# Moving two weight roundings and a bank copy ahead of the last hidden high part at every second turn of the weights

## The reference

```
def swiglu(h, wg, wu, wd):
    return (jax.nn.silu(h @ wg) * (h @ wu)) @ wd

h = rmsnorm(x, p['norm_ffn_pre'][l]) * (1 + sc_f) + sh_f
f = swiglu(h, p['w_ffn_gate'][l], p['w_ffn_up'][l], p['w_ffn_down'][l])
```

## Time and profile before

| | |
|---|---|
| median of 3 runs | 3141.03 us (3135.26 to 3142.76) |
| the profiled execution's own time | 3142.86 us |
| its span, first to last instruction | 3141.1 us |
| TensorE busy | 2906.9 us, 93% of the span |
| VectorE / ScalarE / GpSimd busy | 1744.2 / 1084.2 / 1271.5 us |
| seven-product units, layer 0 | 1214.9 to about 1650 us |
| seven-product units, layer 1 | 2389.0 to about 2825 us |

### The profile page before, as it was taken

One profiled execution on the slowest core, in us unless ns is written; L12 is line 12 of the kernel. 1 busy time (PEld: TensorE's weight loads), 2 busy tenths in 40 slices (PEclk: granted clock), 3 DMA queues, 4 the chain that ended last, 5 costly groups with the idle time before them and its releaser, 6 DMA issues. The chain is left out here.

```text
span 3141.1 us, 60389 instructions
## 1 busy us (share of the span) xinstructions
PE 2906.9 (93%) x24873; PEld 2617.4 (83%) x24873; DVE 1744.2 (56%) x3025; ACT 1084.2 (35%) x2178; POOL 1271.5 (40%) x899
## 2 busy tenths in 40 slices
PE   6999899899899898999999998898888999999997
PEld 4888576566566898999999997888888999999996
DVE  4331245465556477666654237787477666664234
ACT  5411136421112454333331015575464333331012
POOL 2411157633333453444443114586553444443112
PEclk8999989888889999999999999999999999999998
DMA  9455300255554332233237322311332223247322
GB/s 313 165 201 181 103 22 1 91 178 180 182 182 162 96 99 70 98 111 106 90 131 259 130 85 83 87 29 30 90 107 70 93 102 111 85 140 249 140 79 79
DMA packets 241597, 377.89 MB, mean 120 GB/s; under 512 B 15530, under 2 KB 156203, under 8 KB 241060
## 3 DMA queue, kind: packets, MB, share of 16 engines
q1 hardware_dynamic: 200092, 253.95, 24.5%
q0 software_dynamic: 20992, 75.51, 7.2%
q10 hardware_dynamic: 20240, 44.57, 3.9%
HBM read 298.71 MB, written 73.28 MB: 118 GB/s over the span
## 5 line engine op out<-in xcount | busy, mean ns | idle before, releaser
L791 PE MATMUL ps<-HS,w_split 128*128 128x272 f32 x1920 | 269.6, 290 | 12.4 <-ACT sg L1048 10.0
L807 PE MATMUL ps<-HS,w_ring 128*128 128x272 f32 x1920 | 274.7, 290 | 0.0
L791 PEld LDWEIGHTS ps<-HS,w_split 128*128 128x128 f32 x1920 | 250.6, 188 | 17.5 <-ACT sg L1048 14.6
L807 PEld LDWEIGHTS ps<-HS,w_ring 128*128 128x128 f32 x1920 | 255.5, 190 | 0.0
L2312 PEld LDWEIGHTS ps<-HS_in,w_split 128*128 128x128 f32 x1728 | 222.5, 191 | 27.7 <-issue 16.4
L2312 PE MATMUL ps<-HS_in,w_split 128*128 128x272 f32 x1728 | 233.4, 294 | 9.2 <-DVE HS_in L2531 9.1
L1786 DVE TENSOR_TENSOR Y<-Y,ps 128x272 f32<-128x272 f32 x256 | 112.1, 438 | 224.7 <-PE ps L807 224.7
L1384 POOL TENSOR_TENSOR w_split<-w_raw,w_split 128x512 fp32r<-128x512 f32 x120 | 170.0, 1430 | 120.9 <-ACT w_split L1040 120.9
L762 PE MATMUL ps<-HS,w_ring 128*128 128x272 f32 x1344 | 186.4, 301 | 26.5 <-PEq L156 12.1
L762 PEld LDWEIGHTS ps<-HS,w_ring 128*128 128x128 f32 x1344 | 182.1, 200 | 28.7 <-issue 13.6
L1384 POOL TENSOR_TENSOR w_ring<-w_raw,w_ring 128x512 fp32r<-128x512 f32 x40 | 61.9, 1547 | 282.6 <-ACT w_ring L1040 282.6
(11 more groups left out here) (496 smaller groups left out, 6702.0 us busy)
## 6 DMA issues: line engine op xcount, KB each, us to landing
hid_spill<-hid SPq DMA_DIRECT2D x40, 1088.0 KB, 7.4
w_mod_half<-w_mod_in SPq DMA_DIRECT2D x40, 1024.0 KB
HS<-hid_spill ACTq DMA_DIRECT2D x32, 1088.0 KB, 11.4
w_raw<-w_ffn_gate_in SPq DMA_DIRECT2D x44, 512.0 KB
w_raw<-w_ffn_up_in SPq DMA_DIRECT2D x44, 512.0 KB, 6.0
w_raw<-w_ffn_down_in SPq DMA_DIRECT2D x44, 512.0 KB
x_part<-x_spill SPq DMA_DIRECT2D x54, 272.0 KB, 3.0
x_spill<-Y SPq DMA_DIRECT2D x12, 1088.0 KB, 5.5
```

What stands on the lines that cost most here:

```text
L791: ins = pe.matmul(psum(U.banks(u)[b]), part_slot(j, a)[:, k, :], token_part(n, j, e)[:, k, :], start=(j < 3 and k == 0 and i == 0), stop=( ...
L807: ins = pe.matmul(down_bank(n), slots[DOWN_SLOT[t]][:, a, d * P:(d + 1) * P], hid_cols(k, t, q)[:, e, :], start=(t == lo and j == 0), stop ...
```

## The change

At the turns from an up unit to a gate unit (nine in a layer, after units 3, 7, ... 35; the set `EARLY_COPY` holds the gate unit that follows), ScalarE's stream is put into another order. Before, the order was: high part of hidden quarter 2, high part of hidden quarter 3, high parts of weight operands 5 and 6, copy of the next unit's product 0. Now it is: high part of hidden quarter 2, high parts of weight operands 5 and 6, copy of the next unit's product 0, high part of hidden quarter 3. No instruction is added or removed, and the turns from gate to up stay as they are.

```diff
+EARLY_COPY = [u + 1 for u in Halves.LAST[:-1] if HALF_UNIT[u][2]]
...
-                copy_a(u)
+                if u not in EARLY_COPY:
+                    copy_a(u)
                 first_beside(u, 0)
...
                 finish(2)
+                if soon and mat:
+                    part_high(m + 1, 5)
+                    part_high(m + 1, 6)
+                    copy_a(u + 1)
                 finish(3)
-                if soon:
+                if soon and not mat:
                     part_high(m + 1, 5)
                     part_high(m + 1, 6)
```

## The result

The changed kernel takes 3150.45 us (median of 7 runs, 3145.24 to 3155.62) against 3141.03 us for the kernel before (7 runs, 3135.26 to 3143.72): a ratio of 1.0032, 95% interval 1.0022 to 1.0041, so 9.4 us slower. The forecast was 3155 us within 3132 to 3163.

What follows compares the result with a forecast made beforehand. TensorE, busy 93% of the span, was taken as the bound. Removing 0.76 us and adding 1.48 us at each of 18 turns gave +13.0 us, forecast 3155 us, range 3132 to 3163.

Steps and rivals of the forecast that it cites:

- The gain that the change was to bring: Product 3 at the 18 turns: an earlier copy ends its 0.76 us stall; 14.0 us at most with one longer wait.
- What is late next: At the turns, add_b ends late behind the hidden low parts; product 4 stalls 1.37 us, 1.48 with the refill.
- two insertions: GpSimd's low parts 5 and 6 slip between VectorE's four hidden low parts, adding 2 x 1.1 us per turn.
- the sum: Per turn +1.48 - 0.76 = +0.72 us; over 18 turns +13.0 us.
- The price of an insertion: Each GpSimd low part adds about 1.1 us to VectorE's chain, from rows showing +1.09 and +1.12 us.
- The race of 0.01 us: Whether GpSimd's first low part goes before or after hidden low part 0 doesn't matter; both precede the fourth.
- The reading of the Trainium skill: Each GpSimd low part holds the shared port its full 1.28 us; 0.36 us worse per turn, some 6 us overall.
- the forward move of the loads: SyncE's next weight loads, waiting for low part 6, move about 1 us forward; costed at nothing.
- the sum's two bases: The profiled execution's 3142.86 us, giving 3155.9, and the median of runs shown, 1.8 us lower, giving 3154.
- nothing else happens (1): At the turns, the copy comes early and hidden low parts run undisturbed in 1.49 us; -14 us, 3128 us, chance 0.15.
- One insertion (2): At the turns, only low part 5 goes in, low part 6 following all four; -7 us, 3135 us, chance 0.14.
- Rival 3: Quarter 3's multiply and the copy are held; product 3 stalls 0.4 us again, sum unchanged; chance counted with the forecast.

Runs made afterwards that it cites:

- e3: The changed kernel with VectorE's four hidden low parts at those turns put behind the next unit's add_b and add_e; 3017.97 us, ratio 0.9946.
- e4: The changed kernel with the four hidden low parts' second input read from PSUM, so their values aren't right; 3020.93 us, ratio 0.9950.
- e1: The kernel before with only the copy of product 0 moved ahead of high parts 5 and 6; 3020.47 us, ratio 0.9959.
- e5: The changed kernel with high part 6 held back until after the next gate unit's first sigmoid; 3037.72 us, ratio 1.0011.

## Why the prediction was right

**The gain that the change was to bring** was sized right. It was put at 14.0 us "at most". In the trace of the kernel before the 18 turns lose 14.05 us, in e3 and e4 0.03 us. That their whole stretches are down by 14.0 and 13.9 us too is because differences of 0.2 to 0.3 us elsewhere cancel. That product 3 would start on time, with the copy 0.56 us early, is in the timeline (0.55 us).

**What is late next.** `add_b`, with product 4 behind it, as forecast. Four hidden low parts with two insertions: 1.49 + 2.2 = 3.69 us forecast, 3.68 measured. The stall: 1.37 us forecast, 2.81 - 1.505 = 1.31 measured, since the hidden low parts began 3.25 us after product 0's start, as before, and `add_b` began 0.06 us sooner than worked out. The period from turn to turn went from 1311.74 - 1268.81 = 42.93 us to 1310.99 - 1267.40 = 43.59: +0.66 us where the sum had +0.72. This is the term that was off, and by little: 18 x 0.66 = 11.9 us. The price of an insertion came from rows that bear it, though "normally" is not the word for L1598's 0.69 us: it took that in 20 of its 40 executions and 1.78 us in the other 20.

**What makes it.** e4 shows that it is the second SBUF input, and e1, e5 and the changed kernel give the price for no, one and two low parts. The race of 0.01 us in the prediction was one: both started 0.01 us apart, and as it said, it didn't matter. The reading of the Trainium skill ("SBUF — State Buffer", "Who interferes with whom"), each GpSimd instruction holding the port for its whole length, would have had 1.28 us in place of 1.09, some 7 us more over all turns. The trace agrees with the holding, since each held hidden low part ended 0.30 us after GpSimd's, and not with that price.

**SyncE** is the step whose reasoning was wrong, although it cost the sum little. I called the forward move of the loads worth nothing because of "the slack of a whole gate unit". There was no such slack: VectorE waited 17 times for weights in the kernel before, once for 1.16 us (before 2538.19 us), and at the turn from gate to up that followed product 3 was 0.38 us late. That stall and the smaller ones of the kind are gone, 0.6 us in all; in the other direction, e5 lost some 13 us by it. Together with 0.2 us less in the first units this makes the 11.9 into the 11.1 us seen in the stretches. The median's 9.4 us has an interval of 0.22 to 0.41%, 7 to 13 us, which holds both. The sum's +13.0 us lies at its upper edge. The 3155 us that was said lies between the sum's two bases, 3154 and 3155.9; it is 14 us above the median before and so just outside.

**The rivals.** That nothing else happens (1) is out, by e4 against the changed kernel. One insertion (2) didn't come, since two hidden low parts were long at every turn. Its price, 7 us gained, was too low for the turns, where e5's one insertion gained 10.7 us, and wrong for the whole, which came out no faster: the gain is had only if the weights don't come late. Rival 3, the copy held too, occurred at none of the 18 turns: before product 3 they lose 0.1 us in all.

## What to carry to other kernels

When an engine's work is moved forward, look at what its consumer will then run beside: here ScalarE's earlier rounding released GpSimd, and GpSimd held up VectorE. Before taking a late step forward as a block, move only the part that is awaited (the copy), or take what nobody awaits (the hidden low parts) out of the way of what somebody does. And an instruction that seems to have slack may hold a buffer, as low part 6 did in e5: ask what its end lets begin, in the next stage as well.

## What the runs showed of the hardware

VectorE, with two SBUF inputs, gives up the contended access between two instructions that it issues back to back: a waiting GpSimd instruction goes in after the one that is running, and then a waiting VectorE instruction goes before GpSimd's next. So two queues that are both full alternate: at the turn shown the hidden low parts took 0.43, 1.53, 1.52 and 0.43 us around GpSimd's two. One GpSimd low part of 128 x 512 (1.28 us by itself) costs VectorE 1.09 to 1.10 us, less than its own length, and the two GpSimd instructions lost 0.48 us together (3.04 against 2.56). An add with one SBUF and one PSUM input took 0.43 us right beside it.
